# Hybrid streaming encoder layer, scan stage: queries loaded per chunk with two heads side by side, two-head inverse products, and another order on VectorE

## What is computed

```python
# gated DeltaNet, per chunk; RWKV-7 is brought to the same form by the kernel
t_inv = triangular_solve(lower + eye, eye, lower=True, unit_diagonal=True)
v_new = val_i - einsum('bhcd,bhde->bhce', kc_i, s)
o = einsum('bhcd,bhde->bhce', q_i, s) + einsum('bhij,bhje->bhie', at_i, v_new)
s = s * exp(gl_i)[..., None, None] + einsum('bhcd,bhce->bhde', kt_i, v_new)

# attention: query chunk c reads key chunks c-1 and c
s = einsum('bnikgd,bnjkd->bnkgij', qc, kb) * (SWA_DIM ** -0.5)
s = s - slopes * dist
p = softmax(concatenate([s, sink], -1), axis=-1)[..., :-1]
o = einsum('bnkgij,bnjkd->bnikgd', p, vb)
```

## Time and profile before

| | |
|---|---|
| median of 3 runs | 2027.59 us |
| the profiled execution | 2032.76 us |
| its span, first to last instruction | 2031.0 us |
| TensorE busy | 1942.1 us (96%) |
| VectorE busy | 1051.2 us (52%) |
| ScalarE busy | 568.6 us (28%) |
| GpSimd busy | 552.0 us (27%) |
| mean granted TensorE clock | 0.984 |

### The profile page before, as it was taken

The page is one execution under the profiler, slowest core; times in us unless marked ns, Lnnn a source line. Parts: engine busy times, 40 slices in busy tenths (PEclk is TensorE's granted clock), DMA queues, the critical chain, the costliest instruction groups (busy, mean ns, idle before and its releaser), DMA issues.

```text
span 2031.0 us, 29371 instructions
## 1 busy us (share of the span) xinstructions
PE 1942.1 (96%) x11744; PEld 1570.1 (77%) x11744; DVE 1051.2 (52%) x1379; ACT 568.6 (28%) x888; POOL 552.0 (27%) x336
## 2 busy tenths in 40 slices
PE   8999999999999998989799999999999999999994
PEld 7777787677788887777677777788888888888883
DVE  3747643764379402877677428334343424242437
ACT  3445423334211112444421312221212121221112
POOL 1211212211123223444243734321212121212203
PEclk9999999999999998999899999999999999999997
DMA  6435672345642762766363630321212121212102
GB/s 160 66 97 129 166 183 60 83 117 151 161 127 84 164 206 96 209 197 193 131 202 99 212 108 20 92 62 31 62 31 62 31 62 31 62 31 62 39 13 83
DMA packets 339846, 211.85 MB, mean 104 GB/s; under 512 B 166140, under 2 KB 310140, under 8 KB 337696
## 3 DMA queue, kind: packets, MB, share of 16 engines
q1 hardware_dynamic: 264176, 156.38, 27.9%
q10 hardware_dynamic: 75568, 54.04, 9.2%
HBM read 151.27 MB, written 59.06 MB: 104 GB/s over the span
## 4 chain that ended last, share of the span: by engine, by line
PE 45%; DVE 3%; POOL 2%; DMA 0%; issue 0%; ACT 0%; SPq 0%; DVEq 0%; ACTq 0%
PE b_ps L154 11%; PE b_ps L155 11%; PE b_ps L156 11%; PE f_ps L154 4%; PE f_ps L155 4%; PE f_ps L156 4%; POOL x1lo L1763 1%; DVE l_stats L2276 1%; PE f_ps L1844 1%; DMA o_raw<-in_w_out 0%; DVE y L2288 0%; DVE y L2273 0%; POOL wo_lo L1769 0%; PE f_ps L1881 0%; PE f_ps L1806 0%; POOL x1lo L1755 0%
## 5 line engine op out<-in xcount | busy, mean ns | idle before, releaser
L154 PE MATMUL bank<-xhi,w_hi 128*128 128x512 f32 x976 | 393.3, 403 | 0.5 <-DVE xlo L938 0.5
L156 PE MATMUL bank<-xhi,w_lo 128*128 128x512 f32 x976 | 385.9, 395 | 0.0
L155 PE MATMUL bank<-xlo,w_hi 128*128 128x512 f32 x976 | 385.9, 395 | 0.0
L433 POOL TENSOR_TENSOR w_lo<-w_raw,w_hi 128x1024 fp32r<-128x1024 f32 x61 | 167.4, 2744 | 600.1 <-ACT w_hi L799 600.1
L2248 DVE TENSOR_TENSOR bw_raw<-bw_raw,b_ps 128x512 f32<-128x512 f32 x42 | 28.9, 687 | 388.4 <-PE b_ps L156 380.1
L154 PEld LDWEIGHTS bank<-xhi,w_hi 128*128 128x128 f32 x976 | 183.8, 188 | 45.9 <-issue 3.7
L156 PEld LDWEIGHTS bank<-xhi,w_lo 128*128 128x128 f32 x976 | 183.4, 188 | 44.6
L155 PEld LDWEIGHTS bank<-xlo,w_hi 128*128 128x128 f32 x976 | 183.6, 188 | 44.0 <-issue 1.8
L2256 DVE TENSOR_TENSOR y<-y,f_ps 128x512 f32<-128x512 f32 x320 | 200.5, 683 | 0.5
L1791 POOL TENSOR_TENSOR bw_split<-ff_raw_down,ff_hi_down 128x1024 fp32r<-128x1024 f32 x22 | 53.3, 2423 | 526.7 <-ACT ff_hi_down L2049 526.7
L154 PE MATMUL f_ps<-ff_hi_down,ff_hhi 128*128 128x512 f32 x352 | 142.7, 405 | 3.6 <-DVE ff_hlo L2267 3.6
(11 more groups left out here) (325 smaller groups left out, 3463.8 us busy)
## 6 DMA issues: line engine op xcount, KB each, us to landing
w_raw<-in_w_in ACTq DMA_DIRECT2D x61, 512.0 KB, 4.3
op<-opnd SPq DMA_DIRECT2D x16, 1152.0 KB, 5.5
u<-work ACTq DMA_DIRECT2D x68, 256.0 KB, 3.5
b_gate<-u SPq DMA_DIRECT2D x24, 512.0 KB, 3.5
ff_raw_gate<-in_ffn_gate SPq DMA_DIRECT2D x22, 512.0 KB, 4.0
ff_raw_up<-in_ffn_up SPq DMA_DIRECT2D x22, 512.0 KB, 5.3
ff_raw_down<-in_ffn_down SPq DMA_DIRECT2D x22, 512.0 KB, 5.8
opnd<-work SPq DMA_DIRECT2D x20, 512.0 KB, 5.8
```

Of the source, the lines that this page charges most:

```text
L154: pe.matmul(out, w_hi, x_hi, start=first, stop=False)
L155: pe.matmul(out, w_hi, x_lo, start=False, stop=False)
L156: return pe.matmul(out, w_lo, x_hi, start=False, stop=last)
L433: pool.tensor_tensor(w_lo[b][:, :, :], w_raw[b][:, :, :], as_f32(w_hi[b][:, :, :]), ALU.subtract).then_inc(w_lo_done, 1)
```

## The change

In words:
- Queries are no longer loaded for four chunks at once into `attended`, but per chunk into a cleared tile `query` of 128 partitions x 8 heads x 64, group 0's heads in the upper half of the partitions and group 1's in the lower. Keys are loaded once, in their natural layout. The scores are then four products of 128 rows and 128 columns (two heads) in place of eight of 64x64.
- The corner goes by DMA straight into a cleared `join` of 128 columns, with each of the two matrices of a pair on its own diagonal block. y, z and w are products of both matrices at once: 6, 6 and 4 + 2 products in place of 12, 12 and 8 + 4, with 128 rows and 128 columns; y and z move only 32 columns. y and zt become tiles with 128 columns that are cleared once. `place_inverse` goes; GpSimd writes the upper blocks of zt with two multiplications by a mask, VectorE the lower ones with two fused operations, ScalarE copies y in two parts.
- y and z have places of their own in the PSUM bank, so the wait for zt moves from y to z.
- r_tmp goes: r_g comes from two fused operations, one per column of factors.
- The scaling of the probabilities moves from VectorE (one operation) to ScalarE (four, one for each pair of heads), and the transposes wait for each of them.
- VectorE has an order of its own, `VECTOR_TURNS`: s_sum, sum and reciprocal, s_g and sv, then zt.
- The early loads of the first three chunks wait for GpSimd's clearing of the three `join` tiles.

The diff, its core:

```diff
-    for k in (0, 64):
-        sp.dma_start(corner[b][k:k + 32, :, :], xinv[c, k:k + 32, 2]).then_inc(inv_landed, 16)
+        sp.dma_start(join[b][k:k + NB, :, k + NB:k + 2 * NB], xinv[c, k:k + 32, 2]).then_inc(inv_landed, 16)
...
+            for b in range(DEEP):
                 pool.memset(join[b][:, :, :], 0.0).then_inc(early_cleared, 1)
-            place_inverse(pool, 0, early, early_join, early_placed)
...
+            sp.wait_ge(early_cleared, DEEP)
             for c in range(DEEP):
                 load_chunk(sp, c, early, opnd, xinv, early_landed, early_inv)
...
+        VECTOR_TURNS = ("state", "attend", "product", "attend", "state", "product", "attend", "state", "attend", "state", "product", "attend")
...
-                sp.dma_start(attended[:, :, t], u[U_SQ * P:(U_SQ + 4) * P, t].rearrange("(j p) t -> p j t", p=P)).then_inc(at_landed[i], 16)
+                sp.dma_start(keys[:, to], u[U_SK * P:(U_SK + 1) * P, t]).then_inc(at_landed[i], 16)
+
+            def load_query(c):
                 for g in range(SKV):
-                    for e in range(2):
-                        sp.dma_start(keys[rwkv_rows(e), g, to], u[U_SK * P + g * SD:U_SK * P + (g + 1) * SD, t]).then_inc(at_landed[i], 16)
+                    at = U_SQ * P + g * 4 * SD
+                    sp.dma_start(query[c % DEEP][g * SD:(g + 1) * SD, 4 * g:4 * g + 4, :],
+                                 u[at:at + 4 * SD, c * C:(c + 1) * C].rearrange("(n d) t -> d n t", d=SD)).then_inc(query_landed[c % DEEP], 16)
...
+                if c < DEEP:
+                    sp.wait_ge(query_cleared, c + 1)
+                load_query(c)
                 if c in (0, 2, 6, 10):
                     load_quarter((c + 2) // 4)
...
-                        last = pe.matmul(ps_y[h, u, :], join[b][h, u, :], inv[b][h, 0, u, :], start=True, stop=True)
+                    last = pe.matmul(ps_y[:, u, :], join[d][:, u, :], packed[d][:, 0, u, :], start=True, stop=True)
...
-                        last = pe.matmul(ps_z[h, u, :], y[b][h, u, :], inv[b][h, 1, u, :], start=True, stop=True)
+                    last = pe.matmul(ps_z[:, u, :], y[b][:, u, :], packed[d][:, 1, u, :], start=True, stop=True)
...
-                        pe.matmul(ps_w[h, j * C:(j + 1) * C], zt[b][h, j, :], r_rw[b][h, j, :], start=True, stop=True)
+                    pe.matmul(ps_w[:, j * C:(j + 1) * C], zt[b][:, j, :], r_rw[b][:, j, :], start=True, stop=True)
...
-                        last = pe.matmul(at_s[h, j, :], attended[h, j, c * C:(c + 1) * C], keys[h, j // 2, c * C:c * C + W], start=True, stop=True)
+                    two_heads = query[c % DEEP][:, 2 * j:2 * j + 2, :].rearrange("p n s -> p (n s)")
+                    last = pe.matmul(at_s[:, j, :], two_heads, keys[:, c * C:c * C + W], start=True, stop=True)
...
-                dve.tensor_tensor(zt[b][:, :, :], ps_z, inv[b][:, 1, :, :], ALU.add).then_inc(zt_done, 1)
+                for e in range(2):
+                    h = rwkv_rows(e)
+                    dve.scalar_tensor_tensor(zt[b][h, :, lower_of(e)], packed[d][h, 1, :, :], tab("lower")[h, :], ps_z[h, :, :],
+                                             ALU.mult, ALU.add).then_inc(zt_done, 1)
...
+                for p in range(2):
+                    dve.scalar_tensor_tensor(r_g[b][:, p, :], ps_r[:, 256 + p * GD:256 + (p + 1) * GD], cols[:, c, 2, p:p + 1],
+                                             tok_g[b][:, 1, p, :], ALU.mult, ALU.add).then_inc(r_g_done, 1)
...
-                act.activation(y[b][:, :, :], ps_y, ACT.Copy).then_inc(y_done, 1)
+                for e in range(2):
+                    act.activation(y[b][lower_of(e), :, 64 * e:64 * e + NB], ps_y[lower_of(e), :, :], ACT.Copy).then_inc(y_done, 1)
...
-                act.wait_ge(r_tmp_done, c + 1)
+                act.wait_ge(r_g_done, c * 2 + 2)
...
+                act.wait_ge(rested, 2 * c + 2)
+                for j in range(4):
+                    act.activation(score[b][:, j, :], score[b][:, j, :], ACT.Copy, scale=rest[b][:, j:j + 1]).then_inc(p_done, 1)
...
+            for b in range(2):
+                pool.memset(zt[b][:, :, :], 0.0).then_inc(zt_cleared, 1)
...
+                for e in range(2):
+                    h = rwkv_rows(e)
+                    pool.tensor_scalar(zt[b][h, :, 64 * e:64 * e + NB], packed[d][h, 1, :, :], tab("upper")[h, :], None, ALU.mult).then_inc(inv_done, 1)
```

More of the change, by code:

```diff
@@ L78, in constants @@
     put("causal_again", t >= s)
+    put("upper", s < 32)
+    put("lower", s >= 32)
     put("corner", (s < 32) & (t >= 32))
@@ L259, in scan_tiles @@
     op, ar, sv, wv = loads("op", [N_FLAT]), loads("ar", [8, 2, C]), loads("sv", [8, C]), loads("wv", [8, C])
-    packed, corner = loads("inv_packed", [2, NPAIR, NB]), loads("inv_corner", [NPAIR, NB])
-    inv, join = ([sb(f"{name}{b}", [P] + shape) for b in range(2)] for name, shape in (("inv", [2, NPAIR, C]), ("join", [NPAIR, C])))
-    return op, ar, sv, wv, packed, corner, inv, join
+    packed, join = loads("inv_packed", [2, NPAIR, NB]), loads("join", [NPAIR, P])
+    return op, ar, sv, wv, packed, join
 def load_chunk(sp, c, tiles, opnd, xinv, landed, inv_landed):
-    op, ar, sv, wv, packed, corner, inv, join = tiles
+    op, ar, sv, wv, packed, join = tiles
     b, row = c % DEEP, opnd[c]
@@ L434, in _ @@
             local.sweep(pool)
-            *_, inv, join = early
+            *_, join = early
             pool.wait_ge(inv_stored, 16 * 4 * R)
-            for b in range(2):
-                pool.memset(inv[b][:, :, :, :], 0.0).then_inc(early_cleared, 1)
+            for b in range(DEEP):
                 pool.memset(join[b][:, :, :], 0.0).then_inc(early_cleared, 1)
-            pool.wait_ge(early_cleared, 4)
-            pool.wait_ge(early_inv, 48)
-            place_inverse(pool, 0, early, early_join, early_placed)
-            pool.wait_ge(early_placed, 4)
+            pool.wait_ge(early_cleared, DEEP)
         @block.sync
@@ L1188, in scan_and_attend, with run @@
         of = lambda e: slice(4 * e, 4 * e + 4)
-        def run(product, state, attend):
+        def run(product, state, attend, turns):
             first = product(0)
@@ L1359, in sum_values @@
                 last.then_inc(mm_pv, 1)
-            run(product, state, attend)
+            run(product, state, attend, TURNS)
             sum_values(NCH - 1)
@@ L1412, in state @@
                     last.then_inc(s_g_done, 1)
-                yield
                 dve.wait_ge(s_sum_done, c * 2 + 2)
@@ L1444, in attend @@
                 dve.reciprocal(rest[b][:, :], rest[b][:, :]).then_inc(rested, 1)
[L1445 to L1446 removed]
                 yield
                 yield
[L1450 removed]
+            run(product, state, attend, VECTOR_TURNS)
         @block.scalar
@@ L1550, in state @@
                 yield
-            run(product, state, lambda c: iter(()))
+            run(product, state, lambda c: iter(()), TURNS)
             local.sweep(pool)
```

101 lines of the change are left out of this document (47 added, 54 removed).

## The result

The changed kernel took 2047.91 us (median of 4 runs, 2045.49 to 2053.23) against 2028.37 us before: a ratio of 1.010, 95% interval 1.0075 to 1.0124. It is 19.5 us slower where 5.3 were forecast, and outside the range of 2021 to 2043.

A forecast was written before the change was run, and what follows sets the result against it. TensorE, busy 96% of the span, was taken as the bound. 13 chunks x 0.3 = 4.0, start 3.2, chunks 14 and 15 -0.45 and -1.5 gave +5.3 us: 2032.9 us, range 2021 to 2043.

The forecast's parts named there:

- Edits that I cost at nothing: Side edits priced at zero: mask multiplications, fused r_g, query DMAs, and early loads starting some 2 us later.
- TensorE's side: Scan products with 128 stationary columns: scores +0.07, w +0.34, values and y +0.35, z +0.61, together +1.37 us a chunk.
- the price taken from L667: Each new 128-column pass on TensorE costs 0.112 us, with 32, 64 or 128 moving columns alike.
- Rival 3: TensorE weight loads are hidden, so fewer products save time: period 10.8 us, -18 us, 2010; 10% with similar smaller gains.
- The stall at the transposes: TensorE's 1.2 us wait per chunk before transposing the scores goes, through VectorE's new order and scaling on ScalarE.
- rival 2: ScalarE's copies and scaling become the new wait before z or the transposes: +12.6 us on top, about 2045; 18%.
- The lock on sv: Second sv multiplication waits for GpSimd's s_dec on the shared ports: 0.13 us a chunk, bounds 0 and 0.5.
- The start of the scan: Later values and low-clock y and z delay the first state step 3.9 us; 0.7 returns: plus 3.2, bounds 0 to 6.
- Rival 1: The scan's start and the lock on sv cost nothing: about +1 us, 2028.6; 27%.
- chunk 1's 0.3: Forecast addition to each undisturbed chunk's period: 11.97 to 12.27 us, including 0.13 for sv.
- The end: Last scan chunks: chunk 14 minus 0.45 us, chunk 15 minus 1.5 (bounds minus 3 and plus 1.5).

The follow-up runs named there:

- first experiment: Changed kernel with the three clearings of join moved from GpSimd to VectorE, the wait kept: 2038.52 us, 9.4 us below the changed kernel.
- second experiment: Kernel before, with only the early loads' wait for GpSimd's clearings added: 2036.25 us, ratio 1.0045, 8.4 us slower.
- fifth experiment: Kernel before, with only the two unused mask columns added to the constant tables, shifting later tiles by 8 bytes: 2032.82 us, ratio 1.0024.
- the sixth: Same kernel as the first experiment plus 62 spare table columns, so tiles move by 256 bytes in place of 8: 2035.59 us, ratio 1.0035.
- fourth experiment: Same kernel as the first experiment, but values and keys of the first four chunks load ahead of the first query: 2036.57 us, ratio 1.0045.

## Why the prediction was wrong, point by point

**The step that failed.** Under "Edits that I cost at nothing" stands: "The early loads of the first three chunks now wait for three clearings of join, 768 elements each; one of that size takes 0.74 us at 767.87, so they start some 2 us later, with the scan's start at 789.45 as their due time." I took the duration from the earlier trace rows and passed over its start. The clearing sits at 767.87 us, behind the last weight split in GpSimd's program, and the loads that now wait for it ran at 711.30; of SyncE's queue in that stretch the prediction has no row. With both starts the working is short: the loads begin at about 770, need the 30 us that they took from 711.30 on, end at about 800, and the scan starts some 10 us late. Measured: 9.7 in the trace, 9.4 and 8.4 in the times of the first two experiments. With this term the forecast would have been 2042, inside its own range.

**A part that was not in the sum.** The two table columns were not thought of as an edit with a price. They cost 4.1 us in the pair that resolves it (fifth experiment), 2.9 by the medians of the other. No row of before could have shown that, but the shift of the tiles could be read in the whole diff. With it the forecast comes to 2045 to 2046, against 2047.91.

**TensorE's side: right.** TensorE in the chunk from 854.11 us, which answers the earlier trace rows:

```profile
857.08 1.16 PE L1334 MATMUL ps_at<-at_keys,at_query 128*128 128x128 f32 x8
858.07 1.00 PE L1287 MATMUL ps_w<-r_rw,zt 128*128 128x64 f32 x8
...
859.41 0.27 PE L1254 MATMUL ps_yz<-tables,at_values 128*128 128x128 f32 x1
859.52 1.42 PE L1257 MATMUL ps_yz<-inv_packed,join 128*128 128x32 f32 x12
860.88 0.69 PE L1296 MATMUL ps_r<-wv,op 128*64 128x64 f32 x16
...
862.13 1.53 PE L1265 MATMUL ps_yz<-inv_packed,y 128*128 128x32 f32 x12
863.59 0.34 PE L1313 MATMUL ps_o<-sv,ar 128*64 128x64 f32 x4
...
866.13 0.66 PE L1276 MATMUL ps_r<-s_g,op 128*64 128x128 f32 x8
```

Scores 0.99 (1.00 forecast), w 1.34 (1.34), values and y 1.47 (1.46), z 1.46 (1.45); together +1.38 (+1.37). The 12 passes of y take 1.36 us, 0.113 each: the price taken from L667 holds for 32 moving columns as for 2. Rival 3, hidden weight loads, is out. The Trainium skill, "TensorEngine Tiling (Array Packing)", Instruction Overhead, by which few moving columns would cost about 60 cycles a product, does not hold as the pitch of these float32 products with 128 stationary columns; the measurement decides.

**The stall at the transposes: right.** In chunks 1 to 14 it went entirely, and rival 2's mechanism did not occur there. ScalarE's two copies of y took 0.67 us for two (0.33 each forecast) and the four scaled copies 1.28 (0.27 to 0.39 each forecast), and TensorE's only wait for them was in chunk 0: 0.29 us, and the four transposes behind it took 1.14 us instead of 0.58. There ScalarE loads a table for 1.28 us (ACT_TABLE_LOAD at 824.70) ahead of the exponentials, and everything behind comes late. That rival 2's time of 2045 lies near the measurement is chance: another wait made it.

**The lock on sv: mis-sized, no cost but once.** VectorE and GpSimd, two rounds, after:

```profile
853.11 1.16 DVE L1416 TENSOR_TENSOR sv<-s_sum,plast 64x256 f32<-64x256 f32 x1
...
863.61 0.16 DVE L1441 TENSOR_TENSOR at_rest<-at_rest,at_own 128x4 f32<-128x4 f32 x1 [0.49 <-ACT at_score L1498]
...
864.69 1.60 DVE L1416 TENSOR_TENSOR sv<-s_sum,plast 64x256 f32<-64x256 f32 x2
```

```profile
864.92 1.09 POOL L1555 TENSOR_TENSOR s_dec<-s_g,egl_bc 128x512 f32<-128x512 f32 x1 [8.04 <-DVE s_g L1409]
```

As forecast, the row sum no longer meets s_dec (0.16 us), and the second sv multiplication does: 1.16 us in place of 0.43. But both have ended by 866.29 (864.69 + 1.60), and TensorE wants them 0.49 us behind the row at 866.13, at 866.62, so the 0.13 us of the sum were not spent, but for 0.3 us in chunk 1, behind the late chunk 0: a period of 12.02, where the forecast without the lock was 12.14. The other 0.12 are two smaller things: the wait that went was 1.23 by start distances, and the two r groups run 0.09 us faster. The Trainium skill's page "SBUF — State Buffer" says that the loser of the pair of ports blocks for a whole instruction; 1.16 against 0.43 beside a GpSimd instruction of 1.09 agrees in kind: the multiplication ends at 866.29, 0.28 behind the GpSimd instruction.

**The start of the scan: right in kind, too small.** The first state step comes 4.87 us later, forecast 3.9. z costs the 1.2 more that were forecast at the lower clock level (2.67 us up to the state step, 1.47 before), y with its copy 1.2. The difference is in the values, which come 5.34 us after the scan's start (2.90 before): 2.4 later, forecast 1.5. SyncE issues them 1.5 us later, as forecast, but the issue itself takes 1.32 us behind the two query DMAs (804.53) instead of 0.34 (789.79).

Chunk 0 then takes 15.04 instead of 13.20, where I had expected it to give back 0.7. The lower level reaches further into it: the granted clock is 0.53 from 814.74 to 820.80 and 1.00 from there to 829.78. So a and the scores still run low (0.62 and 1.52 us, against 0.39 and 0.92 before), while w, y and z cost there what they cost in any chunk (1.34, 1.47 with the values, 1.45), and the transposes come late as said above. Start, chunk 0 and chunk 1 together cost 7.0 us, against a forecast of 3.5 (3.2 and chunk 1's 0.3). Rival 1, by which start and lock cost nothing, had the lock right and the start wrong.

**The end: right.** Chunk 14 -0.70 us (-0.45 forecast), chunk 15 from its first state step to the last product -1.58 (12.95 to 11.37; -1.5 forecast).

**The scan as a whole** is 3.8 us longer in the traces, or 5.4 us if two long chunks of the kernel before are set aside (12.43 us, which comes back as 12.43 and 12.70 in the fifth and second experiment, and 13.16, which no other profile has); forecast +5.3. That agreement is two errors against each other, and so luck: chunks 2 to 13 cost 0.6 in place of 3.6, and the start with chunks 0 and 1 7.0 in place of 3.5. The part that I worked out was right to 2 us in sum. What lay outside it, a wait and two columns, carried another 12 to 13.

## What to carry to other kernels

When an edit adds a wait to a queue, read three starts and not only a duration: when the waiting instruction ran so far, where in its engine's program the releasing one stands, and how long the chain behind the wait is. A transfer that ran 45 us ahead of need has no due time until it is put behind something late. And when a change is a bundle, cost its halves apart: here one half gained 20 us and the other lost 40 (28 by its products and the queries, 9 by the wait and 3 by the shifted tiles), and only the gain was worth keeping.

## What the runs showed of the hardware that I had not expected

- **Tiles 8 bytes off make transfers land later.** Four writes of 256 KB to DRAM that took 4.2 us to land in five kernels took 5.7 to 6.3 in the four kernels in which the tiles lie 8 bytes further; a shift of 256 bytes leaves 4.2. A finer split into packets isn't it: the pages of the kernel before and of the fifth experiment count the same 339846 packets, with the same numbers under each size, and those of the first and the sixth both 350848. The same packets land later; by what way the address does it, no run tells.
- **How long TensorE stood says little of the clock that it gets back.** With the products of before, a stand of 3.2 us was followed by a granted clock of 0.56 up to the first state step and 0.85 in chunk 0, one of 13.1 us (second experiment) by 0.66 and 1.00. With the new products it was 0.50 and 0.86 behind 3.2 us (first experiment), 0.50 and 0.81 behind 12.9. The two kinds differ in what follows: in the second experiment TensorE stands 0.17 us for the values and 0.9 for the copy, in the changed kernel 2.63 and 1.15. Without most of the wait for the values (fourth experiment, 0.22 us) it was 0.51 and 0.85, so that wait alone isn't it; the rest no run separates.
- **A change of shape costs 0.1 to 0.15 us** between groups: the scores up to the next group take 1.08 us when 64*64 follows and 0.99 when 128*128 does; a transpose before y takes 0.26 us before 64*64 products and 0.11 before 128*128.
